# Hybrid decoder step on one core: routed experts taken largest first, six weight fetches made while routing, scaled rows in two buffers

## The reference, cut to what matters

```python
def _moe_ffn(h, w_router, b_router, w_e1, w_e3, w_e2, w_s1, w_s3, w_s2):
    aff = jax.nn.sigmoid((h @ w_router).astype(jnp.float32))          # (tokens, 64 experts)
    _, eidx = lax.top_k(aff + b_router.astype(jnp.float32), 6)
    gsel = jnp.take_along_axis(aff, eidx, axis=-1)
    gates = gsel / jnp.sum(gsel, -1, keepdims=True) * 2.5
    ...   # for every token and each of its 6 experts e:
    y = _swiglu(h_pad[tok], w_e1[e], w_e3[e], w_e2[e])                # w_e1, w_e3: 1024x256, w_e2: 256x1024
    routed = sum over the token's experts of gate * y
    return routed + _swiglu(h, w_s1, w_s3, w_s2)                      # the shared expert
```

## Time and profile before

| | |
|---|---|
| median of 3 runs | 2773.03 us |
| the profiled execution | 2762.65 us |
| its span in the trace | 2760.7 us |
| routing (first to last instruction of `route_phase`) | 1529.9 to 1678.8 us |
| expert steps on TensorE | 1696.5 to 2682.5 us |
| busy over the span | PE 79%, DVE 34%, ACT 24%, POOL 15% |
| mean granted TensorE clock | 0.868 |

### The profile page before, as it was taken

How to read it: one execution, slowest core, us unless ns; L and a number is a source line. 1 busy time by engine, 2 the same in 40 slices (tenths; PEclk the granted TensorE clock), 3 DMA queues, 4 the chain that set the end, 5 groups by cost and what they waited for, 6 DMA issues and landing times. The chain is left out here.

```text
span 2760.7 us, 29445 instructions
## 1 busy us (share of the span) xinstructions
PE 2184.2 (79%) x9232; PEld 1135.0 (41%) x9233; DVE 944.5 (34%) x2090; ACT 650.1 (24%) x1361; POOL 422.8 (15%) x586
## 2 busy tenths in 40 slices
PE   5899907877476888996998874988988888978885
PEld 1566806521245664343765531333333333333332
DVE  5100084599698423224533521111111111111116
ACT  2100002256578432114211110111111111111114
POOL 0000030010000000000233053222222222212120
PEclk8899957987557899998888896999999999999897
DMA  9400010010000032423215136966786688877756
GB/s 367 181 0 0 1 48 5 6 39 23 0 1 1 0 126 110 164 93 138 69 69 194 34 132 249 318 229 224 263 291 221 215 311 296 272 285 250 278 155 261
DMA packets 88149, 408.41 MB, mean 148 GB/s; under 512 B 22087, under 2 KB 27163, under 8 KB 59132
## 3 DMA queue, kind: packets, MB, share of 16 engines
q1 hardware_dynamic: 59284, 293.27, 27.7%
q0 software_dynamic: 27552, 109.65, 14.0%
q10 hardware_dynamic: 1232, 4.46, 0.4%
HBM read 352.35 MB, written 64.09 MB: 151 GB/s over the span
## 5 line engine op out<-in xcount | busy, mean ns | idle before, releaser
L2925 PE MATMUL psum<-wx,hT_x 128*64 128x512 f32 x2208 | 513.2, 619 | 135.1 <-DMA wx<-in_w_e 135.1
L2925 PEld LDWEIGHTS psum<-wx,hT_x 128*64 128x64 f32 x2208 | 174.7, 143 | 467.1 <-issue 466.6
L2851 DVE COPY hT_x<-psum 128x512 f32<-128x512 f32 x69 | 47.7, 692 | 632.4 <-PE psum L2912 632.4
L2962 PE MATMUL psum<-wx,hidT_x 128*64 128x512 f32 x1104 | 252.1, 598 | 1.3 <-ACT hidT_x L2868 1.3
L2868 ACT COPY hidT_x<-psum 128x256 f32<-128x256 f32 x69 | 25.7, 372 | 568.1 <-PE psum L2948 568.1
L2291 PE MATMUL psum<-wx 128*128 128x512 f32 (+1 forms) x288 | 139.7, 648 | 1.4 <-PEq L1970 1.4
L2902 DVE TENSOR_SCALAR y_x<-psum,slot_gate 128x512 f32<-128x512 f32 x69 | 51.8, 750 | 232.8 <-DMA scr_acc<-y_x,add_idx 128.8
L2962 PEld LDWEIGHTS psum<-wx,hidT_x 128*64 128x64 f32 x1104 | 73.1, 136 | 128.0 <-issue 118.2
L2841 POOL DMA_INDIRECT scr_acc<-y_x,add_idx x69 | 110.7, 1604 | 33.9 <-issue 33.9
L1672 PE MATMUL psum<-ident,sm 128*128 128x128 f32 x288 | 53.3, 320 | 74.2 <-ACT sm L1624 47.6
L2875 ACT ACTIVATE y_x<-psum,slot_gate 128x512 f32<-128x512 f32 x69 | 47.4, 687 | 260.8 <-DMA scr_acc<-y_x,add_idx 141.8
(11 more groups left out here) (655 smaller groups left out, 3391.0 us busy)
## 6 DMA issues: line engine op xcount, KB each, us to landing
wx<-in_w_e SPq DMA_DIRECT2D x198, 1024.0 KB, 11.3
wa<-in_w_ada SPq DMA_DIRECT2D x8, 3072.0 KB, 14.0
xt<-in_x_prompt SPq DMA_DIRECT2D x16, 512.0 KB, 5.7
f<-scr_acc SPq DMA_DIRECT2D x16, 512.0 KB, 11.1
scr_acc<-zero SPq DMA_DIRECT2D x11, 512.0 KB, 16.2
w<-in_w_in SPq DMA_DIRECT2D x1, 5392.0 KB, 25.0
wx<-in_w_out SPq DMA_DIRECT2D x2, 2048.0 KB, 12.3
scr_x<-x POOLq DMA_DIRECT2D x8, 512.0 KB, 3.0
```

Of the source, the lines that this page charges most:

```text
L2925: mm = pe.matmul(psum[at, 2 + par, :].rearrange("p (j f) -> p j f", j=2), hT[:, par, k, at], w13[:, :, k], start=(k == 0), stop=(k == KD - 1))
L2962: mm = pe.matmul(psum[at, 5 + c, :], hidT[:, k, at], w2[:, k, c * 512:(c + 1) * 512], start=(k == 0), stop=(k == 1))
```

## The change

Four things change. First, the order of the experts. A key of 64 times the pieces minus the expert's number is compared between all pairs of experts; one small matmul, placed behind up(2) of the shared expert, sums for each expert the pieces of all that have a larger key. This takes the place of the running sum, so pieces are laid out from the expert with most pieces to that with fewest, equal ones by number. The queues are still 23 consecutive pieces each. Second, SP fetches ranks 0 to 5 in `route_phase`, rank 3 and on after the shared expert's last down projection; ACT's queue loads the slot table. Third, `y` has two buffers, taken in turn, and the additions are still made one after another. Fourth, `load_final` stands behind the loop of fetches.

```diff
+            for rank in range(QUEUES):
+                if rank >= 2:
+                    sp.wait_ge(wx_land[rank % 2], 48 * (rank // 2))
+                if rank == PRE:
+                    sp.wait_ge(dn_ps, NTL)
                 fetch(rank)
...
+            act.wait_ge(scattered, 16 * TOPE * NTL)
+            act.dma_start(st[:], scr["slots"].rearrange("(b p) c -> b p c", p=P)).then_inc(st_land, 16)
...
-            seq(nc.vector.tensor_tensor_scan(inc[:], one[:], nb[:], 0.0, ALU.mult, ALU.add))
-            nc.vector.tensor_tensor(exc[:], inc[:], nb[:], ALU.subtract)
+            seq(nc.vector.scalar_tensor_tensor(key[:], nb[:], float(EXPERTS), number[:], ALU.mult, ALU.subtract))
+            diag = cst["ident"][0:EXPERTS, 0:EXPERTS]
+            seq(nc.vector.scalar_tensor_tensor(junk_e[0:EXPERTS], key[0:EXPERTS], 1.0, diag, ALU.mult, ALU.mult,
+                                               accum_out=key_at[0:EXPERTS]))
+            seq(nc.vector.scalar_tensor_tensor(junk_e[0:EXPERTS], nb[0:EXPERTS], 1.0, diag, ALU.mult, ALU.mult,
+                                               accum_out=nb_at[0:EXPERTS]))
+            nc.vector.tensor_scalar(more[:], key[0:EXPERTS], key_at[0:EXPERTS], None, ALU.is_lt)
+            nc.vector.tensor_scalar(spread[:], cst["ones"][0:EXPERTS], nb_at[0:EXPERTS], None, ALU.mult
+                                    ).then_inc(more_made, 1)
+            dve.wait_ge(exc_ps, 1)
+            seq(nc.vector.tensor_copy(exc[:], psum[:, 7, 0:EXPERTS]))
+            seq(nc.vector.tensor_tensor(inc[:], exc[:], nb[:], ALU.add))
+            seq(nc.vector.tensor_reduce(total[:], inc[:], AX, ALU.max))
...
             for c in range(2):
...
+                seq(nc.vector.scalar_tensor_tensor(key[:], inc[:], at, number[:], ALU.is_gt, ALU.mult))
+                seq(nc.vector.scalar_tensor_tensor(junk_e[:], exc[:], at, key[:], ALU.is_le, ALU.mult,
+                                                   accum_out=want[:, c, 0:1]))
...
+                if i == 1:
+                    pe.wait_ge(more_made, 1)
+                    pe.matmul(psum[:, 7, 0:EXPERTS], spread[:], more[:], start=True, stop=True).then_inc(exc_ps, 1)
...
-        y = sb("y_x", [P, D])
+        y = sb("y_x", [P, 2, D])
...
-            for rank in range(PRE, QUEUES):
-                e = load(sp, T_EXP + rank, 0, EXPERTS - 1)
-                sp.wait_ge(w_land[rank % 2], 48 * (rank // 2))
-                fetch_expert(sp, a, wx, e, rank, w_land[rank % 2])
-            load_final(sp, a, scr, w_next)
             count = load(sp, T_FETCHES, 0, FETCHES)
...
+            load_final(sp, a, scr, w_next)
...
-            pool.dma_start(spare[:], scr["acc"][TRASH:TRASH + P, 0:2]).then_inc(added, 16)
+            for c in range(2):
+                pool.dma_start(spare[:, 2 * c:2 * c + 2], scr["acc"][TRASH:TRASH + P, 0:2]).then_inc(added, 16)
...
-                pool.wait_ge(added, 16 * b + 16)
+                pool.wait_ge(added, 16 * b + 32)
...
                 act.wait_ge(added, 16 * b + 16)
-                nc.scalar.activation(y[:, 0:512], psum[:, 5, :], ACT.Copy,
+                nc.scalar.activation(y[:, par, 0:512], psum[:, 5, :], ACT.Copy,
```

More of the change, by code:

```diff
@@ L2415, in route_phase @@
         want = sb("r_want", [P, 2, 3])
+        number, key, key_at, nb_at = (
+            sb("r_number", [P, EXPERTS]), sb("r_key", [P, EXPERTS]), sb("r_key_at", [P, 1]), sb("r_nb_at", [P, 1]))
+        more, spread = sb("r_more", [EXPERTS, EXPERTS]), sb("r_spread", [EXPERTS, P])
         junk_e, junk_t = sb("junk_e", [P, EXPERTS]), sb("junk_t", [P, TURNS])
@@ L2418, in route_phase @@
         cum, odd, odd_i = sb("r_cum", [1, STEPS]), sb("r_odd", [1, STEPS]), sb("odd_i", [1, STEPS], I32)
+        total = sb("r_total", [P, 1])
         cuts, span = sb("r_cuts", [P, QUEUES - 1]), sb("r_span", [P, 1])
@@ L2429, in route_phase @@
             "chosen", "cnt_ps", "steer_made", "meta_made", "scattered", "st_land", "st_ps"))
+        more_made, exc_ps = sem("more_made"), sem("exc_ps")
         change_made, rank_ps, pick_made, pick_ps = (sem(n) for n in ("change_made", "rank_ps", "pick_made", "pick_ps"))
@@ L2527, in _ @@
             nc.vector.tensor_copy(ranks[:], rank_i[:])
+            nc.vector.tensor_copy(number[:], rank_i[:, 0:EXPERTS])
             nc.vector.memset(one[:], 1.0)
@@ L2593, in _ @@
             seq(nc.vector.tensor_scalar(nb[:], nb[:], 1.0 / SUB, None, ALU.mult))
-            seq(nc.vector.tensor_tensor_scan(inc[:], one[:], nb[:], 0.0, ALU.mult, ALU.add))
-            nc.vector.tensor_tensor(exc[:], inc[:], nb[:], ALU.subtract)
-            seq(nc.vector.tensor_scalar(junk_t[:], six[:], inc[:, EXPERTS - 1:], 0.0, ALU.is_lt, ALU.add,
-                                        accum_out=length[:]))
+            seq(nc.vector.scalar_tensor_tensor(key[:], nb[:], float(EXPERTS), number[:], ALU.mult, ALU.subtract))
[11 more added lines that the diff above has]
+            seq(nc.vector.tensor_reduce(total[:], inc[:], AX, ALU.max))
+            seq(nc.vector.tensor_scalar(junk_t[:], six[:], total[:], 0.0, ALU.is_lt, ALU.add, accum_out=length[:]))
             nc.vector.tensor_scalar(change[:], turn[:], length[:], None, ALU.is_lt)
@@ L2819, in _ @@
             pool.wait_ge(idx_put, RING)
-            pool.wait_ge(added, 16)
+            pool.wait_ge(added, 32)
             pool.wait_ge(hg_clear, 1)
@@ L2842, in body @@
                     out=scr["acc"], out_offset=bass.IndirectOffsetOnAxis(ap=si[:, j % 2:j % 2 + 1], axis=0),
-                    in_=y[:], in_offset=None, compute_op=ALU.add).then_inc(added, 16)
+                    in_=y[:, j % 2], in_offset=None, compute_op=ALU.add).then_inc(added, 16)
             blocks(pool, body)
             n = load(pool, T_STEPS, 0, STEPS)
-            pool.wait_ge(added, 16 * n + 16)
+            pool.wait_ge(added, 16 * n + 32)
         def read_hT(eng, copy, half, b_done, par, done):
```

17 lines of the change are left out of this document (8 added, 9 removed).

## The result

The changed kernel takes 2859.40 us (median of 4 runs, 2856.45 to 2864.04) beside 2769.59 us for the kernel before on the same chip: 1.0328 times as long, 95% interval 1.0299 to 1.0357, or +90 us. The forecast was slower, 2841 us, with a range of 2795 to 2885. The time lies in the range; two of its four terms have the wrong sign.

The account below looks back on a forecast made before the run. The prediction took PE's waits for weights (135.1 us), set by when fetches are asked for rather than total bytes, as the bound; 74 - 6 + 0.4 - 0.7 = +68 us on 2773 gave 2841 us, range 2795 to 2885.

Parts of the forecast that it names:

- The order: Expert steps: largest first raises steps with two fetches from 11 to 18; waits +60, slower first matmuls +14, together +74 us.
- doubles: Expert steps with two weight fetches: 11 to become 18, waiting 117, 52 and 7 us by what stands before them.
- singles: Expert steps with one fetch: 38 to become 25, of which 12 wait 1.6 us each, 19 us.
- slower first matmuls: Up projections behind a long wait run slower at first: 40 us in place of 26, +14.
- The window of one step: Expert steps: a weight fetch has one step, 11.8 us, from issue to need, not a whole turn.
- The late turns pile up: Rival, chance 0.12: turns 14 to 21 ask for 3 to 5 fetches each; +105 to +128, about 2890 us.
- The cost goes by fetches in a turn: Rival, chance 0.10: waits follow fetches per turn, not per step; small or no gain and no loss, 2768 us.
- Six fetches while routing: Before the first step: early fetches leave the first gather less contention; -6 us, bounds -8.6 to 0.
- The routing: Routing: new DVE work is covered by PE's up(2), only the new matmul counts; +0.4 us, bounds 0 to +5.
- Two buffers for `y`: Expert steps: only the last step's scaling leaves the path; -0.7 us, bounds 0 and -8.
- The sum: Whole kernel: the four terms add to +68 us on 2773 us, 2841 us.

Follow-up runs that it names:

- the paired kernel: Kernel before with experts largest first and runs of pieces dealt so most and fewest fetches share a step: 0.9900 of the time before, waits 117.9 us.
- The rising order: Kernel before with experts smallest first and runs of pieces dealt so many-expert and few-expert queues share a step: 2725.34 us, 0.9836 of before.
- the two with the scattering held: GpSimd's scattering begun only after the shared expert's last down projection: kernel before, 2789.06 us; the same with early fetches and table load on ACT, 2797.18 us.

## Why the prediction came out as it did

- **The order, +74: right.** The order alone costs 72.5 us. In its trace the 18 doubles wait 173.6 us and 12 singles 19.8, forecast 176 and 19; slower first matmuls are +11.3 us, forecast +14. (In the changed kernel, with the second `y`, they are 181.8, 20.2 and +12.9.) The window of one step, which came from placing each fetch beside the steps, was the mechanism, and the pairing shows it from the other side.
- **The late turns pile up: no.** The longest wait is 13.2 us, and it stands in the second turn. The rival also misread the pattern: of turns 14 to 21 three ask for two fetches, not 3 to 5. **The cost goes by fetches in a turn: no.** The number of fetches is the same in the paired kernel and the waits fall by 75 us.
- **Six fetches while routing, -6: wrong in this kernel, +12 alone.** "Step 2 and its four buffers waited for nothing before" held, and the gain is real where ACT isn't held (-7.7). What failed is that "weights come earlier for nobody" was taken to mean that nobody waits for them. Fetches 3 to 5 wait for the shared expert's last down projection, and with them inside `route_phase` the phase's end waits for their issue, fetch 5's for fetch 3's landing too. The step took that down projection to be early from a trace in which it was, and costed the phase's end at nothing. With ACT held it comes 117 us after the rank matmul in place of 69, SP ends the phase with fetch 5, which costs 8.6 us of the start, and the fetches lie beside the gather as before, so the 6 us are not gained. The slot table's load, moved to ACT's queue behind the last shared output, was costed at nothing in the same way; in the changed kernel it ends 3 us ahead of fetch 5, so how much it would cost alone is not shown.
- **The baseline.** 7.9 us of the +21.1 between the two first traces are ACT's hold, which the kernel before has too in its second trace (one trace with it, one without). One execution was taken for the kernel.
- **The routing, +0.4: not told apart.** DVE's wait for PE shrank as forecast, against this row of the changed kernel's timeline (copy behind the rank matmul, 0.99 us after it in both):

```profile
1566.20 0.23 DVE L2645 COPY r_cum<-psum 1x84 f32<-1x84 f32 x1 [2.76 <-PE psum L2731]
```

- **Two buffers for `y`, -0.7: wrong sign, +8.7 alone.** At the last step the wait for the addition went as forecast, in the changed kernel's timeline:

```profile
2777.29 0.69 ACT L2895 ACTIVATE y_x<-psum,slot_gate 128x512 f32<-128x512 f32 x1 [3.96 <-PE psum L2982]
```

  But the bounds of 0 and -8 left out that additions which leave earlier could meet the weights rather than miss them. The Trainium skill's Best Practices (Trainium Kernel Development and Optimization) recommend double buffering; here PE, which the second buffer was to set free, waited 1.3 us ahead of the down projection in both, and the second buffer cost 0.30%, interval 0.15 to 0.45. The waits of ACT and DVE for additions, which were to be gone, are halved. Waits of the changed kernel (total, times, longest), which answer to the earlier trace rows:

```profile
ACT y_x L2895 <- DMA scr_acc<-y_x,add_idx: 67.3, 21, 3.2
DVE y_x L2922 <- DMA scr_acc<-y_x,add_idx: 61.6, 22, 2.8
```

- **The sum.** +68 was forecast on 2773 us; +90 was measured on 2769.6. The order's term carried it, and the two misses, +18 and +9, both for the worse, come to 27 us where the difference is 22. That 2859 lies in 2795 to 2885 is owed to the width of the order's bounds: the other two terms fell outside their own (+12 where -8.6 to 0 was given, +8.7 where -8 to 0 was).

## What to carry to other kernels

When an expert, a page or a tile has to be fetched into a buffer that comes free one step ahead, count how many fetches fall into the same step, not how many there are or how even they are over a longer turn; dealing long and short runs to the queues in pairs won what sorting lost. Work put ahead of a phase's end makes every engine wait for whatever that work waits for, even if nobody needs its data yet; and a load that gates the next phase belongs on a queue with nothing slow ahead of it. Before a trace is taken for the kernel, look at a second one of the same kernel, and ask where a stage has slack only by luck.

## What the runs showed of the hardware

- ACT is held while GpSimd issues its 54 indirect DMAs (1.26 us each, 67 us): 20 to 33 us, then some 5, then 19 to 23 us, at the same three instructions, with the scattering's start anywhere from 1595.15 to 1604.29, with or without DMA issues on ACT. The rising order shows 13.56, 4.52 and 21.33 us. The DMA engines are all but idle in the gap (2 GB/s at most between 1621 and 1643 in the changed kernel). It did not happen in one trace of 12, nor in the two with the scattering held. What in the issuing does it is open.
- A load of 84 KB took 2.0 us from issue to use with nothing beside it (1675.62 to 1677.62 in the first trace of before) and 8.5 us beside two fetches of 3 MB. The Trainium skill (DMA: Bandwidth & Descriptors, Anatomy of one DMA) gives 2.0 us plus bytes over 436 GB/s, by estimate 2.2 us. Its fit is for a DMA that GpSimd issues, while this load and the fetches of the forecast were issued by SP and ACT; the idle case agrees all the same, the other is not in it.
- A gather of one step's rows to its use took 9.1 us beside fetches and 4.2 us without them.
